# Centring retention's values in their weights, and four norms' column sums as split fp32r

## The chip, the cores and the metric

The kernel runs on one core of a Trainium2 chip. It uses the five engines of the core: TensorE (PE in the profile; its weight loads are PEld), VectorE (DVE), ScalarE (ACT), GpSimd (POOL), and SyncE (SP), which issues most of the DMAs. The metric is the device time of one execution in microseconds (us), as the median of several runs.

## The reference

Two blocks on one sequence of 1,024 positions and 1,024 channels, all in float32. The first block has two layers (a gated convolution, then dilated attention), each followed by a gated side branch; the second has one layer with neighbourhood attention (8 heads) and bidirectional retention (4 heads of 128 value channels) side by side, and an MLP. What the change touches is the mean square that each norm takes over the channels, and the norm behind retention, which takes a head's mean away:

```python
def rms_norm(x, g):
    y = x32 * lax.rsqrt(jnp.mean(x32 * x32, axis=-1, keepdims=True) + EPS)
    return y * g
...
def head_group_norm(y, gain):            # y: (batch, seq, heads, 128)
    mu = jnp.mean(y, axis=-1, keepdims=True)
    var = jnp.mean(jnp.square(y - mu), axis=-1, keepdims=True)
    y = (y - mu) * lax.rsqrt(var + EPS)
    return y.reshape(bsz, seq, heads * dv) * gain
...
    proj = h @ w_in[l]
    na_q, na_k, na_v, r_q, r_k, r_v, r_g = jnp.split(proj, splits, axis=-1)
    ret = bidirectional_retention(rq, rk, rv, ...)      # linear in rv
    ret = head_group_norm(ret, ret_norm_gain[l])
    ret_out = jax.nn.silu(r_g) * ret
```

## The kernel before

**Layout.** Activations stand transposed: 8 tiles of 128 channels by 1,024 positions, and X, the residual, stays in SBUF. A weight tile is 128 output channels for all 1,024 inputs, [128, 8, 128]. A product of full precision is made of three fp32r products: every operand is split in a rounded high part and the rest (HA, HB: high and low parts of the activations; w_hi, w_lo: of the weights), and hi by hi, lo by hi and hi by lo are added in PSUM. `linear(q, h)` (L878) makes one output tile from weight slot q (0 or 1) in 8 k-parts; each k-part is `products` (L866): 3 fp32r products times 2 halves of 512 positions. Products of plain fp32 operands need two passes where an fp32r product or a transpose needs one.

**Buffers.** PSUM has four tensors of 128x1024: AB (ps_A, ps_B), which `linear` takes in turn, and CD (ps_C, ps_D), taken in turn by everything else. A raw weight tile comes by DMA into w_raw[q]; POOL splits it (`split_weights`, L765: a cast to w_hi at L769, a subtraction to w_lo at L762) as soon as the product before it on that slot has ended; then SP loads the next.

**Order.** Each engine has its own program, and all order between them is by semaphores, written out by hand; the `Tally` class counts their values. An engine runs its list strictly in order, so a wait holds up all behind it.

**Norms.** The squares of the new X are added into ssum tile by tile by DVE (L2314), while the unscaled values times the gain already go into the products; the channels' sum comes from a product of ssum with a matrix of ones, in fp32 (`column_sums`, L889, called by `norm_stats`, L896). ScalarE makes rstd from it (L1490, L1492), and DVE multiplies by rstd when it evacuates a product (`evacuate`, L2354). `opening` (L900) is a stage's first `linear` with `norm_stats` behind it. It begins four stages: the side branches ple0 and ple1, the attention (norm1) and the second block's mixer (mix). In the attention, DVE goes on behind ssum with clearing qT and kT, the angles of the rotation, the evacuation of q and k and their squares' low parts (`square_lo`, L2557), which TensorE sums per head (`head_squares`) from k-part 4 of the third tile on.

**Neighbourhood attention.** Four times, a `linear` for the values, one for the keys, and `neighbourhood` (L1014): 8 units, and in each a k-part of the next tile, then the unit's scores into the other AB tensor. DVE takes the scores out into nsc with the bias and its largest value (`softmax_input`, L2808), ScalarE exponentiates, DVE normalises (L2816, L2819), TensorE turns and multiplies with the values, DVE stores (`take_out`, L2826). TensorE goes on to the tile behind the last unit when the last scores are out (`scores_out`), since it writes to the same PSUM tensor.

**Retention.** Two head pairs (i = 0, 1). Of each, six tiles: rq, rk, two values, two gates. rq of the first pair is the product carried by the last neighbourhood. DVE rotates rq and rk with operands that ScalarE swaps by DMA. The values of a head are turned to positions by channels: `centred_turn` (L1268) multiplies each 128x128 chunk by centre, the unit matrix less 1/128, in fp32, which turns it and takes away the mean over the head's channels at once. Since retention is linear in the values, the mean is then gone from its output. rkT is turned plainly (L1011, by a transpose). `decay_args` makes the table of decays, between ScalarE's exponentials.

## Time and profile before

| | us |
|---|---|
| median of 3 runs | 2422.59 |
| lowest, highest | 2422.40, 2423.52 |
| span of the profiled execution | 2422.7 |
| TensorE busy in it | 2373.7 (98%) |
| DVE, ScalarE, POOL busy | 1617.2 (67%), 1066.1 (44%), 942.1 (39%) |

The span is the time from the first to the last instruction of one execution under the profiler; it differs from the median by 0.1 us. Busy shares are a mean over stages. An engine's idle time costs something only where another waits for it; for TensorE, nearly always busy, every microsecond of waiting is listed with what ended it. Matmuls are pipelined, so a row's duration overlaps the next row's; the time of a product is the distance between starts.

### The profile page before, as it was taken

To read this page: it belongs to the slowest core of one execution; us is meant where nothing else is said; L and a number is where in the kernel's file an instruction comes from. 1 tells how busy PE (TensorE), PEld (TensorE's weight loads), DVE (VectorE), ACT (ScalarE), POOL (GpSimd) and SP (SyncE) were. 2 spreads that over 40 slices of the span, in tenths; PEclk is the share of its full clock that TensorE was granted. 3 is DMA by queue.
4 is the path that set the end of the run, shared out by engine and by line. 5 is a ranking of instruction groups with operands and counts; after the bars stand their busy time and mean duration, and the time that the engine had idled before them with its cause. 6 is when DMAs were issued, how large, how long until landed. Compare 5 with 4: busy or idle time off the path is not lost.

```text
span 2422.7 us, 31585 instructions
## 1 busy us (share of the span) xinstructions
PE 2373.7 (98%) x11548; PEld 1870.4 (77%) x11548; DVE 1617.2 (67%) x2013; ACT 1066.1 (44%) x1630; POOL 942.1 (39%) x528
## 2 busy tenths in 40 slices
PE   9999999999999999999999999999999999999997
PEld 6888648887777777777787777788877888788885
DVE  6999874467647466475856555455688777638985
ACT  5556572235545545456432333223353444444334
POOL 2899912332222222222233111212345455465553
PEclk9999999999999999999999999999999999999999
DMA  3111142221111111111132111221126666876773
GB/s 137 44 43 52 65 182 109 78 87 60 45 40 41 41 40 44 41 40 41 40 100 70 44 41 33 81 78 36 52 113 158 149 159 156 231 293 233 274 250 122
DMA packets 112228, 238.76 MB, mean 99 GB/s; under 512 B 42472, under 2 KB 45416, under 8 KB 112104
## 3 DMA queue, kind: packets, MB, share of 16 engines
q1 hardware_dynamic: 73152, 216.28, 27.8%
q10 hardware_dynamic: 38952, 20.76, 3.9%
q8 instruction: 86, 1.41, 0.2%
q14 instruction: 38, 0.31, 0.0%
HBM read 184.44 MB, written 46.27 MB: 95 GB/s over the span
## 4 chain that ended last, share of the span: by engine, by line
PE 82%; DVE 7%; POOL 3%; ACT 3%; issue 3%; DMA 1%; ACTq 0%; SPq 0%; DVEq 0%; POOLq 0%
PE ps_A L873 24%; PE ps_B L873 23%; PE ps_B L1373 8%; PE ps_A L1373 7%; PE ps_C L1373 4%; PE ps_D L1373 2%; POOL ta L795 1%; PE ps_C L893 1%; PE ps_B L966 1%; PE ps_B L1119 1%; PE ps_C L1011 1%; POOL accp L795 1%; PE ps_D L1011 1%; PE ps_D L1104 1%; PE ps_D L1092 1%
## 5 line engine op out<-in xcount | busy, mean ns | idle before, releaser
L769 POOL CAST w_hi<-w_raw 128x1024 fp32r<-128x1024 f32 x98 | 107.9, 1101 | 1090.4 <-issue 475.9
L762 POOL TENSOR_TENSOR w_lo<-w_raw,w_hi 128x1024 fp32r<-128x1024 f32 x124 | 304.4, 2456 | 50.1 <-ACT w_hi L1513 42.2
L838 POOL TENSOR_TENSOR down_w_lo<-d_raw,down_w_hi 128x512 fp32r<-128x512 f32 x112 | 178.2, 1612 | 141.8 <-ACT down_w_hi L2210 141.8
L873 PE MATMUL ps_A<-HA_hi,w_hi 128*128 128x512 f32 x640 | 201.6, 396 | 4.7 <-POOL w_lo L762 2.2
L873 PE MATMUL ps_B<-HA_hi,w_hi 128*128 128x512 f32 x640 | 202.4, 397 | 2.5 <-POOL w_lo L762 1.5
L873 PE MATMUL ps_A<-HA_lo,w_hi 128*128 128x512 f32 x640 | 197.6, 390 | 0.0
L873 PE MATMUL ps_B<-HA_lo,w_hi 128*128 128x512 f32 x640 | 197.4, 390 | 0.0
L873 PE MATMUL ps_A<-HA_hi,w_lo 128*128 128x512 f32 x640 | 197.3, 390 | 0.0
L873 PE MATMUL ps_B<-HA_hi,w_lo 128*128 128x512 f32 x640 | 197.3, 389 | 0.0
L873 PEld LDWEIGHTS ps_A<-HA_hi,w_hi 128*128 128x128 f32 x640 | 117.1, 188 | 30.8 <-issue 5.0
L873 PEld LDWEIGHTS ps_A<-HA_lo,w_hi 128*128 128x128 f32 x640 | 120.1, 188 | 25.6
L873 PEld LDWEIGHTS ps_B<-HA_lo,w_hi 128*128 128x128 f32 x640 | 120.1, 188 | 25.5
L873 PEld LDWEIGHTS ps_A<-HA_hi,w_lo 128*128 128x128 f32 x640 | 120.1, 188 | 25.5
L873 PEld LDWEIGHTS ps_B<-HA_hi,w_hi 128*128 128x128 f32 x640 | 116.8, 188 | 29.8 <-POOL w_lo L762 2.7
L873 PEld LDWEIGHTS ps_B<-HA_hi,w_lo 128*128 128x128 f32 x640 | 120.1, 188 | 25.4
L1550 ACT ACTIVATE tap_out<-ypad,act_dw 128x1024 f32<-128x1024 f32 x78 | 88.3, 1150 | 96.2 <-POOL accp L795 51.2
L832 POOL TENSOR_TENSOR up_w_lo<-a_raw,up_w_hi 128x512 fp32r<-128x512 f32 x64 | 90.9, 1421 | 77.6 <-ACT up_w_hi L2079 77.6
L3189 DVE TENSOR_TENSOR ht_lo<-t_raw,ht_hi 128x1024 fp32r<-128x1024 f32 x56 | 73.0, 1309 | 69.5 <-ACT ht_hi L2194 69.3
L2210 ACT CAST down_w_hi<-d_raw 128x512 fp32r<-128x512 f32 x112 | 64.5, 618 | 103.6 <-DVE d_raw L3208 39.7
L832 POOL TENSOR_TENSOR up_w_lo<-s,up_w_hi 128x512 fp32r<-128x512 f32 x48 | 72.9, 1520 | 84.3 <-ACT up_w_hi L2079 83.8
L873 PE MATMUL ps_A<-HB_hi,w_hi 128*128 128x512 f32 x320 | 101.8, 399 | 1.2 <-POOL w_lo L762 1.1
L873 PE MATMUL ps_B<-HB_hi,w_hi 128*128 128x512 f32 x320 | 101.7, 399 | 0.0
(489 smaller groups left out, 5926.6 us busy)
## 6 DMA issues: line engine op xcount, KB each, us to landing
w_raw<-w_dram SPq DMA_DIRECT2D x124, 512.0 KB, 3.3
d_raw<-w_dram SPq DMA_DIRECT2D x64, 512.0 KB, 4.5
t_raw<-u_dram SPq DMA_DIRECT2D x56, 512.0 KB, 5.7
a_raw<-w_dram SPq DMA_DIRECT2D x32, 512.0 KB, 7.7
u_dram<-b SPq DMA_DIRECT2D x56, 256.0 KB, 4.9
u_dram<-t SPq DMA_DIRECT2D x48, 256.0 KB, 7.0
X<-x_dram SPq DMA_DIRECT2D x16, 512.0 KB, 6.8
d_raw<-w_dram SPq DMA_DIRECT2D x32, 256.0 KB, 3.0
```

The source lines that it names most:

```text
L762: pool.tensor_tensor(w_lo[q][:, :, :], w_raw[q][:, :, :], w_hi[q][:, :, :].bitcast(F32), ALU.subtract).then_inc(S[f"w_ready{q}"], 1)
L769: pool.tensor_copy(w_hi[q][:, :, :], w_raw[q][:, :, :]).then_inc(S["w_rounded"], 1)
L795: pool.tensor_tensor(accp[u][:, :], (tap_out[0] if j == 0 else accp[u])[:, :], tap_out[(j + 1) % 2][:, :], ALU.add).then_inc(S["pool_tap"], 1)
L832: pool.tensor_tensor(lo[:, :, :], up_source(s), hi[:, :, :].bitcast(F32), ALU.subtract).then_inc(S["up_split"], 1)
L838: pool.tensor_tensor(lo[:, :, :], d_raw[i % 3][:, down_parts(x), :], hi[:, :, :].bitcast(F32), ALU.subtract).then_inc(S["down_split"], 1)
L873: op = pe.matmul(AB[b][:, cols], wt[:, w0 + k, :], act[:, k, cols], start=(first and k == ks[0] and step == 0), stop=(last and k == ks[-1] ...
L893: op = pe.matmul(ps[b][:, cols], m[:, :], src[:, cols], start=first, stop=last)
L1011: op = pe.transpose(CD[b][:, c * P:(c + 1) * P], src(c), ident[:, :])
L1373: op = pe.matmul(bank, a[:, k, :], b[:, k, :], start=(first and k == 0 and step == 0), stop=(k == KH - 1 and step == 2), skip_group_check= ...
L1550: act.activation(tap_out[j % 2][:, :], ypad[u][:, at:at + T], ACT.Identity, scale=act_dw[:, at:at + 1]).then_inc(S["tap_product"], 1)
L2210: act.copy(down_w[i % 3][j][0][:, :, :], d_raw[i % 3][:, down_parts(x), :]).then_inc(S["down_hi"], 1)
L3189: dve.tensor_tensor(dT[t % 4][1][:, ks, :], t_raw[k % 4][:, :, :], dT[t % 4][0][:, ks, :].bitcast(F32), ALU.subtract).then_inc(S["t_ready" ...
```

## The change

**Column sums.** For ple0, norm1, ple1 and mix, ScalarE casts ssum to fp32r (sum_hi), DVE subtracts it from ssum (sum_lo), and TensorE multiplies both with ones in fp32r (`split_stats`). The sum leaves `opening`; in ple0 and ple1 it stands at the head of the second tile, in norm1 and mix ahead of its third k-part.

**Values.** centre and `centred_turn` go; the values are turned by the plain `turn`. The mean over a head's 128 output channels is taken from the weights instead, in w_raw, before POOL splits them: `centre_weights` on DVE, two tiles each time, for the first pair behind unit 6 of the last neighbourhood, for the second behind the evacuation of rqT in the first pair. POOL's loop over these tiles is written out, with a wait for the centred tile in it.

**Semaphores.** Some are merged: the decay's load counts with the diffs, so that ScalarE's first exponential of the decays waits for all four loads; dw_loaded counts in vec_loaded. The renaming of rq_swapped and rk_swapped is left out below.

```diff
+        ones_r = rm.take("ones_r", [P, P], F32R)
+        w_mean = rm.take("w_mean", [P, 2, KT])
...
+        sum_lo, sum_hi = (Region(nc, (at, at + 4 * KB)).take(name, [P, T], F32R)
+                          for name, at in (("sum_lo", free0), ("sum_hi", free0 + 4 * KB)))
...
-            with n.loop(pool, (MLP_AT - W_TILES["conv_in"]) // 2 - 1, w_loaded0=16, w_loaded1=16, lin_done0=1,
+            with n.loop(pool, (RET_AT - W_TILES["conv_in"]) // 2 - 1, w_loaded0=16, w_loaded1=16, lin_done0=1,
                         lin_done1=1, w_rounded=2):
+                split_weights(0)
+                split_weights(1)
+            for pair in range(W_TILES["ret"] // 2):
+                for q in range(2):
+                    if pair % 3 == 1:
+                        pool.wait_ge(S["w_centred"], pair // 3 * 2 + q + 1)
+                    split_weights(q)
...
+            def split_stats():
+                n.next("ssum_added", KT)
+                pe.wait_ge(S["sum_split"], n.next("sum_split"))
+                b = take_cd()
+                for i, part in enumerate((sum_hi, sum_lo)):
+                    op = column_sums(part, ones_r, b, i == 0, i == 1)
+                op.then_inc(S["stats_done"], 1)
...
                 n.next("h_ready", KT)
-                norm_stats()
+
+            def stats_at(at):
+                return lambda k: split_stats() if k == at else None
...
                 opening(0, h)
-                linear(1, h)
+                linear(1, h, pre=stats_at(0))
...
             opening(0, HA)
-            linear(1, HA)
+            linear(1, HA, pre=stats_at(2))
...
-                linear(q ^ 1, HB, pre=rest)
+                linear(q ^ 1, HB, pre=rest or stats_at(2))
...
-                centred_turn(v_in[0])
+                value_turn(v_in[0])
...
+            def round_sum():
+                act.wait_ge(S["ssum_added"], n.now("ssum_added"))
+                act.copy(sum_hi[:, :], ssum[:, :]).then_inc(S["sum_hi"], 1)
...
-            act.wait_ge(S["decay_loaded"], 16)
+            act.wait_ge(S["diffs_loaded"], 4 * 16)
...
+            def split_sum():
+                after("sum_hi")
+                dve.tensor_tensor(sum_lo[:, :], ssum[:, :], sum_hi[:, :].bitcast(F32),
+                                  ALU.subtract).then_inc(S["sum_split"], 1)
...
+            def centre_weights(i):
+                for q in range(2):
+                    mean = w_mean[:, q, :]
+                    dve.wait_ge(S[f"w_loaded{q}"], 16 * ((RET_AT + 6 * i) // 2 + 2))
+                    step(dve.tensor_reduce(mean, w_raw[q][:, :, :], AX.X, ALU.add))
+                    dve.scalar_tensor_tensor(w_raw[q][:, :, :], mean.unsqueeze(2).to_broadcast([P, KT, P]), -1.0 / P,
+                                             w_raw[q][:, :, :], ALU.mult, ALU.add).then_inc(S["w_centred"], 1)
...
                     normalise(u)
+                    if j == PAIRS - 1 and u == 6:
+                        centre_weights(0)
...
                     evacuate(rqT[:, :], 0)
+                    centre_weights(i + 1)
```

On DVE, units 6 and 7 of the last neighbourhood before (nsc: scores, nst: a row's largest value and sum; ISA is the pass that takes scores out of ps_B):

```order
1046 L2819 TENSOR_SCALAR nsc_157<-nsc_157,nst 128x352 [waits dve_step]
1047 L2819 TENSOR_SCALAR nsc_157<-nsc_157,nst 128x352
1048 L2808 ISA nsc_158,nst<-ps_B,bias_154 128x384 [waits turned,scores_done]
1049 L2808 ISA nst 128x1
1050 L2808 ISA nsc_158,nst<-ps_B,bias_156 128x384
```

And the same place in the changed kernel:

```order
1050 L2867 TENSOR_SCALAR nsc_161<-nsc_161,nst 128x352 [waits dve_step]
1051 L2867 TENSOR_SCALAR nsc_161<-nsc_161,nst 128x352
1052 L2815 TENSOR_REDUCE w_mean<-w_raw_54 128x8 [waits w_loaded0]
1053 L2816 SCALAR_TENSOR_TENSOR w_raw_54<-w_mean,w_raw_54 128x1024 [waits dve_step]
1054 L2815 TENSOR_REDUCE w_mean<-w_raw_55 128x8 [waits w_loaded1]
1055 L2816 SCALAR_TENSOR_TENSOR w_raw_55<-w_mean,w_raw_55 128x1024 [waits dve_step]
1056 L2856 ISA nsc_162,nst<-ps_B,bias_158 128x384 [waits turned,scores_done]
```

Four passes over the two value tiles now stand between unit 6's probabilities and unit 7's scores.

On DVE, the end of the sum and the beginning of the attention (norm1) before:

```order
303 L2314 TENSOR_TENSOR ssum<-ssum,sq 128x1024 [waits ssum_added]
304 L182 REGISTER_ALU
305 L182 COMPARE_AND_BRANCH
306 L2705 MEMSET qT 128x1024
307 L2705 MEMSET kT 128x1024 [waits dve_step]
```

And in the changed kernel:

```order
304 L2344 TENSOR_TENSOR ssum<-ssum,sq 128x1024 [waits ssum_added]
305 L182 REGISTER_ALU
306 L182 COMPARE_AND_BRANCH
307 L2355 TENSOR_TENSOR sum_lo<-ssum,sum_hi 128x1024 [waits sum_hi]
308 L2743 MEMSET qT 128x1024
```

The subtraction, with its wait for ScalarE's cast, stands ahead of everything that DVE does for the attention.

## Rows read from the trace of the kernel before

**Rows 1.** The page, part 4: the chain that ended last, by engine.
```profile
PE 82%; DVE 7%; POOL 3%; ACT 3%; issue 3%; DMA 1%; ACTq 0%; SPq 0%; DVEq 0%; POOLq 0%
```

**Rows 2.** Timeline, mix: start, duration, engine, line, operation, count [idle before <- releaser].
```profile
1303.23 1.88 PE L893 MATMUL ps_C<-ssum,ones 128*128 128x512 f32 x4
1305.41 0.62 PE L873 MATMUL ps_B<-HB_lo,w_hi 128*128 128x512 f32 x2
```

**Rows 3.** Timeline, beginning of the attention (norm1), four engines.
```profile
549.30 1.22 DVE L2314 TENSOR_TENSOR ssum<-ssum,sq 128x1024 f32<-128x1024 f32 x1
...
552.82 2.91 DVE L2581 CAST turns<-pos_i 128x1024 f32<-128x1024 int32 x1
...
569.99 1.23 DVE L2557 TENSOR_TENSOR k_lo<-k_sq,k_hi 128x1024 fp32r<-128x1024 f32 x1
...
561.63 1.05 ACT L1705 CAST q_hi<-q_sq 128x1024 fp32r<-128x1024 f32 x1
...
564.29 1.36 POOL L769 CAST w_hi<-w_raw 128x1024 fp32r<-128x1024 f32 x1 [9.11 <-issue]
...
571.27 0.73 PE L893 MATMUL ps_C<-k_hi,head_r 128*128 128x512 f32 x2 [0.78 <-DVE k_lo L2557]
```

**Rows 4.** Timeline, TensorE, retention: turns of the values and of rkT.
```profile
1559.88 1.10 PE L1011 MATMUL ps_C<-ident,rkT 128*128 128x128 f32 x8 [1.35 <-DVE rkT L2912]
...
1645.30 1.95 PE L1273 MATMUL ps_D<-centre,mix 128*128 128x128 f32 x16
1647.08 1.04 PE L1011 MATMUL ps_C<-ident,rkT 128*128 128x128 f32 x8
1647.87 0.71 PE L873 MATMUL ps_B<-HB_hi,w_hi 128*128 128x512 f32 x2
```

**Rows 5.** Timeline, beginning of ple1: the last add and the sum.
```profile
1209.69 1.23 DVE L2314 TENSOR_TENSOR ssum<-ssum,sq 128x1024 f32<-128x1024 f32 x1
...
1214.43 1.88 PE L893 MATMUL ps_D<-ssum,ones 128*128 128x512 f32 x4
```

**Rows 6.** Timeline, retention: DVE and POOL at the same time.
```profile
1636.89 3.41 DVE L2911 TENSOR_TENSOR r_m<-r_m,rsin 128x1024 f32<-128x1024 f32 x1
...
1635.88 3.34 POOL L762 TENSOR_TENSOR w_lo<-w_raw,w_hi 128x1024 fp32r<-128x1024 f32 x1
```

**Rows 7.** Timeline, last neighbourhood, units 6 and 7: DVE, TensorE, POOL.
```profile
1518.52 0.72 DVE L2819 TENSOR_SCALAR nsc<-nsc,nst 128x352 f32<-128x352 f32 x2
1519.85 0.56 DVE L2808 CUSTOM_DVE_ANT_0 nsc<-ps_B,bias 128x384 f32<-128x384 f32 x1 [0.62 <-PE ps_B L1058]
...
1520.34 0.55 DVE L2808 CUSTOM_DVE_ANT_0 nsc<-ps_B,bias 128x384 f32<-128x384 f32 x1
...
1521.17 0.71 PE L873 MATMUL ps_B<-HB_hi,w_hi 128*128 128x512 f32 x2
...
1519.13 1.04 POOL L769 CAST w_hi<-w_raw 128x1024 fp32r<-128x1024 f32 x1 [24.35 <-PE ps_A L873]
```

**Rows 8.** Timeline, one row; and groups by line: busy us, mean ns | idle before.
```profile
1201.31 1.28 DVE L2307 SCALAR_TENSOR_TENSOR HA_lo<-X,vec,HA_hi 128x1024 fp32r<-128x1024 f32 x1 [0.23 <-ACT HA_hi L1502]
...
L2611 DVE TENSOR_REDUCE least<-st_x 128x16 f32<-128x48 f32 x4 | 0.9, 214 | 0.0
```

**Rows 9.** Timeline, DVE, retention, behind the evacuation of rqT.
```profile
1618.70 1.23 DVE L2942 TENSOR_TENSOR r_m<-r_m,sd_sq 128x1024 f32<-128x1024 f32 x1 [8.01 <-ACT sd_sq L2053]
```

**Rows 10.** Timeline, TensorE, MLP; and a stretch: length, busy by engine, PEclk, DMA, GB/s.
```profile
1824.73 0.51 PE L1373 MATMUL ps_B<-ht_hi,up_w_hi 128*128 128x512 f32 x1 [1.90 <-DVE b L3072]
...
1826.00:1829.40 3.40, 3.40 (x10) 2.64 (x9) 1.99 (x4) 2.72 (x6) 3.40 (x3) 0.52 1.03 186
```

**Rows 11.** Timeline, retention's first pair: DVE and POOL.
```profile
1537.86 1.03 DVE L2874 COPY lg<-lg 64x4 f32<-64x4 f32 x2 [1.32 <-ACT lg L1973]
...
1556.64 1.22 DVE L2911 TENSOR_TENSOR r_m<-r_m,rsin 128x1024 f32<-128x1024 f32 x1
...
1556.91 1.84 POOL L769 CAST w_hi<-w_raw 128x1024 fp32r<-128x1024 f32 x1 [7.35 <-issue]
```

More of the change, by code:

```diff
@@ L389, in build @@
         TAB_X, TAB_Z = RET_HEADS * P, 2 * RET_HEADS * P
-        centre = rr.take("centre", [P, P])
         lg = rr.take("lg", [P, 4, RET_HEADS])
@@ L1266, in chunk, with value_turn @@
                 return t[rows, c * P:(c + 1) * P]
-            def centred_turn(v):
-                b = take_cd()
-                pe.wait_ge(S["centre_ready"], 1)
-                for c in range(BLOCKS):
-                    op = pe.matmul(chunk(CD[b], c), chunk(v, c), centre[:, :], start=True, stop=True)
-                op.then_inc(S["v_turned"], 1)
+            def value_turn(v):
+                turn(lambda c: chunk(v, c), BLOCKS)[1].then_inc(S["v_turned"], 1)
             def chunk_states(h):
@@ L1530, in _ @@
             act.wait_ge(S["ssum_added"], DVE_SQUARES - 1)
-            act.dma_start(dw_sb[:, :, :], dw).then_inc(S["dw_loaded"], 16)
+            act.wait_ge(S["ones_loaded"], 16)
+            act.copy(ones_r[:, :], ones[:, :])
+            act.dma_start(dw_sb[:, :, :], dw).then_inc(S["vec_loaded"], 16)
             norm_stats()
@@ L1686, in _ @@
                 .then_inc(S["pos_loaded"], 16)
+            round_sum()
             norm_stats()
@@ L1908, in _ @@
             load_rows(1)
+            round_sum()
             norm_stats()
@@ L1957, in _ @@
                 act.wait_ge(S[f"cd_free{b}"], n.now(f"cd_free{b}"))
-            act.dma_start(lg[:, 0:2, :], decay).then_inc(S["decay_loaded"], 16)
+            act.dma_start(lg[:, 0:2, :], decay).then_inc(S["diffs_loaded"], 16)
             at = (BLOCKS - 1) * P
@@ L2014, in _ @@
                 act.wait_ge(S[f"ab_free{b}"], n.now(f"ab_free{b}"))
-                swap_halves("rq_swapped", qs, rqT)
+                swap_halves("q_swapped", qs, rqT)
                 after_ab()
-                swap_halves("rk_swapped", r_m1[0], rkT)
+                swap_halves("k_swapped", r_m1[0], rkT)
                 pass_ab(2)
@@ L2702, in pair @@
                 gated(j)
+            split_sum()
             for dst in (qT, kT):
@@ L2867, in decay_args @@
             def decay_args():
-                dve.scalar_tensor_tensor(centre[:, :], ones[:, :], -1.0 / P, ident[:, :], ALU.mult,
-                                         ALU.add).then_inc(S["centre_ready"], 1)
                 after("gamma_ready", 2)
@@ L2877, in decay_args @@
                     dve.tensor_copy(lg[high, 3, e::2], lg[high, 1, 1 - e::2])
-                after("diffs_loaded", 3 * 16)
+                after("diffs_loaded", 4 * 16)
                 apart, toward = steps[:, 0:P], steps[:, P:2 * P]
@@ L2951, in _ @@
                     decay_args()
-                turned_pair("rq_swapped", rqT, qs, "rq_ready")
+                turned_pair("q_swapped", rqT, qs, "rq_ready")
                 evacuate(mix[:, i * 2 + PAIRS, :], 0)
-                turned_pair("rk_swapped", rkT, r_m1[0], "rk_ready")
+                turned_pair("k_swapped", rkT, r_m1[0], "rk_ready")
                 evacuate(mix[:, i * 2 + 1 + PAIRS, :], 1)
```

13 lines of the change are left out of this document (9 added, 4 removed).

## The prediction

> **What bounds the kernel now.** I read the page's chain of waits first: 82% of the span runs through TensorE [rows 1], so TensorE time saved counts in full and a TensorE wait added counts in full, unless a wait that is already there takes it up. Then the list of TensorE's own waits: there are few, and the change stands beside two of them, one of 0.78 us at the first attention tiles, before 571.27 [rows 3], and one of 1.35 us in the retention stage [rows 4]. So the question is what the change takes off TensorE, and where the added VectorE (DVE) work makes TensorE wait. The profiled execution's span is 2422.7 us and the median of the runs 2422.6, so the two can be taken as one; I sum against 2422.6.
>
> **Column sums of four norms (ple0, norm1, ple1, mix).** From the sum's first pass at 1303.23 to the products' second pair at 1305.41 are 2.18 us; one pair of products in it takes 0.455 us, so the four fp32 passes of the sum take 1.73 us [rows 2]. In fp32r the sum is four passes as well (high and low part, two halves each), at the 0.227 us of a product, 0.91 us together: 0.82 us less for each norm.
>
> The new chain is: last add into ssum, ScalarE's cast to sum_hi (1.05 us, as the cast of the same shape [rows 3]), DVE's subtraction (1.22 us), TensorE. For ple1 the last add ends at 1210.92, so the low part is there at about 1213.3, and TensorE asks at 1214.43 [rows 5]: hidden with 1.1 us to spare; uncovered it would cost those 2.3 us. ple0 has more room. For mix the sum is asked for two k-parts (2.7 us) after 1303.23 [rows 2], and the masks and biases that DVE does behind the subtraction have idle time after them. Three norms: -2.5 us.
>
> **norm1 is different**, because DVE has a full list behind the sum. Its last add ends at 550.52 [rows 3]. DVE waits for the cast until 551.6 and subtracts until 552.9; the low part is ready 2.4 us after the last add and the sum's new place is two k-parts (2.7 us) behind the old one, so TensorE doesn't wait there. But the whole list behind it (clearing qT and kT, the angles, the evacuations, the low parts q_lo and k_lo) is 2.3 us late. The conversion of the positions took 2.91 us at 552.82 [rows 3], of which I put over 2 us down to standing still beside a subtraction of GpSimd (POOL); so about 1.0 of the 2.3 us vanishes there and 1.35 us stay. Then POOL's next split, 564.29 before [rows 3], comes 0.8 us earlier, because TensorE does, and DVE's list is later: its cast and subtraction (some 1.0 and 2.4 us) now fall ahead of q_lo instead of beside the evacuation of k_in. Laid out operation by operation, k_lo ends at about 574.1 where it ended at 571.22, and TensorE goes on at 574.2 instead of 571.27 [rows 3]. So here the 0.82 us are lost and 2.9 us come on top. Bounds: +1.4 (only the first shift) and +3.3 (nothing vanishes at the conversion). I take +2.9, since the two-SBUF operations in this trace do stand still beside POOL [rows 6].
>
> **Turns of the values.** The product with centre takes 16 passes and 1.78 us (1645.30 to 1647.08), a plain turn 8 passes and 0.79 us (1647.08 to 1647.87) [rows 4]: 0.99 us less, four times. The first of the four is followed by the 1.35 us wait for rkT [rows 4], whose chain (ScalarE's loads, decay arguments, swaps) doesn't get shorter; that wait grows by 0.99 us and nothing is won. Three count: -3.0 us. Nothing else that I find waits in their place: the second turn is followed by score products whose operands have been there for microseconds.
>
> **Centring in the last neighbourhood unit.** This is the term that decides. After the probabilities of unit 6 (1518.52 + 0.72 = 1519.24) DVE goes to the scores of unit 7 at 1519.85 and gives them free at 1520.9; TensorE starts the rk tile at 1521.17, in the very bank that those scores stood in [rows 7]. Only 0.6 us of idle time is there. Now two reductions and two products over 128x1024 stand between. A product of this kind (scalar_tensor_tensor) is 1.28 us, a reduction of 48 elements a partition 214 ns [rows 8]; no row shows one of 1,024. I bound it by 0.9 us (the 1.28 us less a third) and 1.3 us, and take 1.2: 0.16 us fixed, worked out from the short one, and 1.06 us for the elements, as in the 1.22 us passes (such as [rows 9]). Two tiles: about 4.85 us, from 1519.15 to 1524.0. Scores free at 1525.0, TensorE at 1525.1 instead of 1521.17: +3.95 us (bounds 3.3 and 4.3). What is queued behind on DVE: unit 7's scores and probabilities, the evacuation of rqT, both needed microseconds later. ScalarE's loads for the retention stage wait for unit 7's output, which comes from TensorE, so the rkT chain shifts along and its wait doesn't take the stall up. POOL's split of the first value tile, 1519.13 before [rows 7], waits for the centred tile until 1521.7; TensorE needs it at about 1539: hidden, at 13 us.
>
> The second centring stands in an idle stretch of DVE of 8.01 us before 1618.70 [rows 9]; 4.85 us fit: nothing. POOL's split there is late by 4 us against 14: nothing. ScalarE now waits for all four loads instead of the decay's before its first exponential, about 0.75 us later; but the first copies of lg behind it took 1.03 us for four columns each, from 1537.86 [rows 11], standing beside POOL's subtraction, so I take 0, bounds 0 and 0.7. Dropping the centre matrix (0.28 us) is ahead of the same stand: 0. The rounded ones and the unrolled POOL loop lie in idle time: 0.
>
> **TensorE's clock.** In the products of the MLP TensorE stood still 1.90 us before 1824.73, and from 1826.0 to 1829.4 the granted clock was 0.52, its 1.2 GHz level, with 10 products in 3.40 us [rows 10]: (1 - 0.52) x 3.40 = 1.6 us lost. After the 1.35 us wait [rows 4] it stayed at 2.4 GHz. The change makes two waits much longer than 1.90: 3.95 us at 1521, and some 4.6 us in two pieces at 569 to 574. TensorE is the bound behind both, so I count 1.6 us for each, 3.3 together (bounds 0 and 4.8). The wait for rkT becomes 1.35 + 0.99 = 2.3 us, a little over the one that was followed by the low level; with one case to go by I take half of it, 0.8.
>
> **Sum.** -2.5 + 2.9 - 3.0 + 3.95 + 3.3 + 0.8 = +5.5 us: 2428.1 us. What a measurement of this kernel can tell from no change is about 0.2%, 4.8 us.
>
> **Rivals.**
>
> *POOL gets ahead of DVE (slower still).* DVE operations with two SBUF inputs and POOL's passes take turns in this trace: rkT's product with the sines lasted 3.41 us at 1636.89, until POOL's w_lo (1635.88, 3.34) had ended [rows 6]. In the centring, POOL starts its cast when the first tile is centred, and DVE asks for its second product some 1.15 us later, just as that cast ends. By my durations DVE is ahead of POOL's w_lo by 0.1 us; if the reduction takes over 1.3 us it is behind, and waits 2.4 us more: 2430.5. The same can happen at rkT, where DVE (1556.64) is ahead of POOL's cast (1556.91) by 0.27 us [rows 11]: 2.7 us more, 2430.8, or 2433.2 with both. Chance 0.2.
> The Trainium skill, "SBUF — State Buffer", section "Who interferes with whom", says that whichever of the two issues first holds the shared ports for the whole instruction, that a tensor_reduce never takes them on trn2, and that an operation with two SBUF inputs does. By that rule, the trace agrees at 1636.89, the reductions are safe and the second product alone is at stake, which is this rival.
>
> *The centring and the splits are covered (faster).* If TensorE didn't need the scores' bank before DVE is back, and norm1's list had slack, all that is left is 3.3 us from the sums and 3.0 us from the turns: 2416.3. It decides at one point, whether DVE's detour at 1519 ends within about 0.9 us of its old time. For it speaks only that DVE is idle 1 to 2 us in each unit; against it that the idle time lies ahead of unit 7 only with 0.6 us. Chance 0.1.
>
> *The clock stays at 2.4 GHz.* The stalls come as worked out, and no low stretch follows: 2422.6 + 1.4 = 2424.0. For it: only one low stretch in the trace; against it: the waits are twice as long as the one before it. Chance 0.15.
>
> **How the numbers follow.** My forecast has 0.55, its own range 2425.5 to 2429.8 (norm1 by its bounds, none to two and a half low stretches). The range over all: 2421.5 to 2432.5; it leaves out the covered case and the case of both collisions with POOL. Slower by over 0.2% means above 2427.4: all of the POOL rival and about 0.6 of the forecast, 0.53. Faster: 0.10. Within: 0.37.
>
> **What would show it.** Right: a TensorE wait of about 4 us for DVE's nst (L2856 after) just ahead of the rk tile; two low-clock stretches of 3.4 us; the k sum of the first head_squares some 3 us later against the tile before it; column sums of 0.9 us; turns of 0.8 us; DVE idle before L2990 shrunk from 8.0 to about 3. Wrong: TensorE going on at once after unit 7, which would leave only gains; or reductions far from 1.2 us, which move the stall by twice the difference.

## The result and the profile after

| | before | after |
|---|---|---|
| median, us | 2423.28 | 2428.05 |
| lowest, highest, us | 2422.40, 2425.45 | 2425.90, 2434.80 |
| span of the profiled execution, us | 2422.7 | 2426.7 |

The ratio is 1.0019, 95% interval [1.001, 1.0028]: 4.8 us slower, just about the smallest difference that can be told from none. Both kernels ran eight times in this comparison. One slow execution of after, 7354.05 us, whose cause is not known, is left out of the ratio and of the highest value and counts in the median alone, which is 2427.95 without it. The other seven runs of after spread three times as wide as those of before, and that turns out to be part of the answer.

The page after, parts 1 and 4. TensorE is still 98% busy and the chain's shares are those of [rows 1], so every row below is about where TensorE stands still or runs slowly.

```profile
PE 2368.9 (98%) x11516; PEld 1868.4 (77%) x11516; DVE 1631.2 (67%) x2024; ACT 1071.1 (44%) x1635; POOL 951.9 (39%) x528
...
PE 82%; DVE 7%; POOL 3%; ACT 3%; issue 3%; DMA 1%; ACTq 0%; SPq 0%; DVEq 0%; POOLq 0%
```

TensorE's waits after (line, what it waited for: us in total, times, longest). The first is new. The second was 0.78 us [rows 3], the third 1.35 us [rows 4].

```profile
PE ps_B L885 <- DVE nst L2856: 3.6, 1, 3.6
PE ps_C L905 <- DVE k_lo L2594: 3.5, 1, 3.5
...
PE ps_C L1035 <- DVE rkT L2960: 2.5, 1, 2.5
```

**The stall at the last neighbourhood unit.** Timeline after, DVE, POOL and TensorE; it answers to [rows 7]. Between the probabilities of unit 6 (L2867) and the scores of unit 7 (L2856) stand two reductions of 1.21 us and two products of 1.22 us, 4.78 us from 1522.24 to 1527.02. POOL's cast starts behind the first centred tile, and its subtraction (1526.02) behind DVE's second product (1525.87), 0.15 us apart: DVE stayed ahead.

```profile
1521.61 0.72 DVE L2867 TENSOR_SCALAR nsc<-nsc,nst 128x352 f32<-128x352 f32 x2
1522.24 1.21 DVE L2815 TENSOR_REDUCE w_mean<-w_raw 128x8 f32<-128x1024 f32 x1
1523.48 1.22 DVE L2816 SCALAR_TENSOR_TENSOR w_raw<-w_mean,w_raw 128x1024 f32<-128x1024 f32 x1
1524.63 1.21 DVE L2815 TENSOR_REDUCE w_mean<-w_raw 128x8 f32<-128x1024 f32 x1
1525.87 1.22 DVE L2816 SCALAR_TENSOR_TENSOR w_raw<-w_mean,w_raw 128x1024 f32<-128x1024 f32 x1
1527.02 0.55 DVE L2856 CUSTOM_DVE_ANT_0 nsc<-ps_B,bias 128x384 f32<-128x384 f32 x1
...
1526.02 3.30 POOL L765 TENSOR_TENSOR w_lo<-w_raw,w_hi 128x1024 fp32r<-128x1024 f32 x1
...
1528.11 1.22 PE L885 MATMUL ps_B<-HB_hi,w_hi 128*128 128x512 f32 x2 [3.60 <-DVE nst L2856]
```

**norm1.** Timeline after, beginning of the attention; it answers to [rows 3]. DVE waits for ScalarE's cast and subtracts (550.92). The conversion of the positions took 1.64 us where it had taken 2.91, but q_lo took 3.42 us, because POOL's subtraction had begun 0.39 us before it. k_lo ended at 572.69, and TensorE, which asked at 569.28, stood still for 3.46 us.

```profile
550.92 1.22 DVE L2355 TENSOR_TENSOR sum_lo<-ssum,sum_hi 128x1024 fp32r<-128x1024 f32 x1 [1.12 <-ACT sum_hi L1522]
...
554.45 1.64 DVE L2618 CAST turns<-pos_i 128x1024 f32<-128x1024 int32 x1
...
564.61 3.42 DVE L2594 TENSOR_TENSOR q_lo<-q_sq,q_hi 128x1024 fp32r<-128x1024 f32 x1
...
571.46 1.23 DVE L2594 TENSOR_TENSOR k_lo<-k_sq,k_hi 128x1024 fp32r<-128x1024 f32 x1 [0.44 <-ACT k_hi L1734]
...
564.22 2.72 POOL L765 TENSOR_TENSOR w_lo<-w_raw,w_hi 128x1024 fp32r<-128x1024 f32 x1
...
572.74 1.22 PE L905 MATMUL ps_C<-k_hi,head_r 128*128 128x512 f32 x2 [3.46 <-DVE k_lo L2594]
```

**The clock.** Stretches of after: length, TensorE busy (count), granted clock, DMA share, GB/s. At both waits the clock fell to 0.50, the 1.2 GHz level, for 6.8 us each time: from 571.3 to 578.1 and from 1527.1 to 1533.9, so that it was already low for the last 1.4 and 1.1 us of the waits. The 0.60 and 0.57 below are means over stretches that are a little longer. Behind the MLP's wait of 1.9 us, where the kernel before had its only low stretch [rows 10], it did not. The last row is for later: 1,005 products in 228 us of the MLP.

```profile
569.30:571.30 2.00, 0.00 (x0) 1.00 0.21 84
571.40:578.10 6.70, 5.36 (x13) 0.50 0.28 40
...
572.50:579.50 7.00, 6.76 (x19) 0.60 0.24 34
1526.50:1534.50 8.00, 6.39 (x16) 0.57 0.19 66
1824.00:1840.00 16.00, 14.09 (x62) 1.00 0.73 179
1850.00:2078.00 228.00, 228.00 (x1005) 1.00 0.61 151
```

**The retention stage.** Timeline after. A turn of values takes 0.87 us to the next, where the product with centre took 1.78 us [rows 4]. DVE's idle time ahead of L2990, with the second centring in it, has shrunk from 8.01 us [rows 9] to 3.23.

```profile
1569.76 1.09 PE L1035 MATMUL ps_C<-ident,rkT 128*128 128x128 f32 x8 [2.46 <-DVE rkT L2960]
...
1654.27 1.03 PE L1035 MATMUL ps_D<-ident,mix 128*128 128x128 f32 x8
1655.14 1.04 PE L1035 MATMUL ps_C<-ident,rkT 128*128 128x128 f32 x8
...
1627.67 1.23 DVE L2990 TENSOR_TENSOR r_m<-r_m,sd_sq 128x1024 f32<-128x1024 f32 x1 [3.23 <-ACT sd_sq L2083]
```

**The account.** The table gives, for the same TensorE instruction in each profiled execution, its start less its start in the first trace of the kernel before. A change from row to row is what that stretch cost or gave. "Late", "fp32" and "both" are kernels of the next section.

| instruction (start before) | before, 2nd | after | after, 2nd | late | fp32 | both |
|---|---|---|---|---|---|---|
| second tile behind ple0's sum, 464.71 | -0.40 | -0.71 | -0.89 | -0.99 | -0.76 | -0.92 |
| norm1, k sum, 571.27 | -0.40 | 1.47 | 1.28 | 1.18 | -0.78 | -0.95 |
| attention, 620.39 | -0.39 | 4.32 | 3.09 | 3.06 | -0.78 | -0.96 |
| attention, 899.75 | -0.18 | 4.62 | 3.34 | 3.29 | -0.73 | -1.01 |
| behind ple1's sum, 1216.61 | -0.20 | 3.91 | 2.71 | 2.60 | -1.53 | -1.79 |
| behind mix's sum, 1307.70 | -0.19 | 3.08 | 1.89 | 1.77 | -2.36 | -2.62 |
| rk tile, 1521.17 | -0.30 | 6.94 | 5.80 | 1.71 | 1.43 | -2.62 |
| turn of rkT, 1559.88 | -0.29 | 9.88 | 7.43 | 4.40 | 6.12 | -2.54 |
| second pair's scores, 1660.73 | -0.32 | 7.15 | 4.66 | 4.18 | 5.92 | -5.28 |
| MLP, 1825.31 | -0.28 | 7.21 | 4.69 | 4.57 | 6.22 | -5.23 |
| MLP, 1853.80 | -0.26 | 5.53 | 3.00 | 4.14 | 5.81 | -6.90 |
| MLP, 2058.36 | -0.26 | 4.24 | 1.71 | 2.85 | 4.51 | -8.20 |
| last norm's sum, 2405.46 | -0.97 | 3.96 | 0.60 | 1.83 | 4.10 | -8.23 |

### The profile page after: what moved, and what is told of

The parts are those of the page before. It is cut to its first block, busy times and chain, and to the rows that moved or that the text cites. A ratio compares the mean times of both kernels' runs of the same rounds, so it can differ in the third digit from the quotient of the medians.

```text
span 2426.7 us, 31507 instructions
## 1 busy us (share of the span) xinstructions
PE 2368.9 (98%) x11516; PEld 1868.4 (77%) x11516; DVE 1631.2 (67%) x2024; ACT 1071.1 (44%) x1635; POOL 951.9 (39%) x528
## 4 chain that ended last, share of the span: by engine, by line
PE 82%; DVE 7%; POOL 3%; ACT 3%; issue 3%; DMA 1%; ACTq 0%; SPq 0%; DVEq 0%; POOLq 0%
PE ps_A L885 24%; PE ps_B L885 24%; PE ps_B L1393 8%; PE ps_A L1393 7%; PE ps_C L1393 4%; PE ps_D L1393 2%; POOL ta L798 1%; PE ps_C L905 1%; PE ps_B L990 1%; PE ps_B L1143 1%; PE ps_C L1035 1%; PE ps_D L1035 1%; POOL accp L798 1%; PE ps_D L1128 1%; PE ps_D L1116 1%
## 5 line engine op out<-in xcount | busy, mean ns | idle before, releaser
L844 POOL TENSOR_TENSOR up_w_lo<-s,up_w_hi 128x512 fp32r<-128x512 f32 x48 | 79.5, 1659 | 71.1 <-ACT up_w_hi L2109 70.0
```

Of the source, the lines that this page charges most:

```text
L844: pool.tensor_tensor(lo[:, :, :], up_source(s), hi[:, :, :].bitcast(F32), ALU.subtract).then_inc(S["up_split"], 1)
```

## The experiments

My theory: the stall at unit 7 and the one for k_lo make up the loss, each with a low clock behind it, over gains of 5 to 6 us. Rivals: the low clock isn't the waits'; the cost lies elsewhere in the retention stage.

Ratios below are against the kernel before, run beside each kernel; differences from after are between medians of different comparisons. After's interval was [1.001, 1.0028]. Those of the kernels with one edit overlap or touch it, so their medians alone prove little and the readings rest on their traces; the kernels with both edits are clear of it.

### Centring the first pair late

```diff
-                    if j == PAIRS - 1 and u == 6:
-                        centre_weights(0)
...
                     evacuate(rqT[:, :], q)
+                    centre_weights(0)
                 take_out(6)
```

> The changed kernel with one move: the first pair of value tiles is centred behind the evacuation of rqT, where VectorE stands idle, instead of between the probabilities of unit 6 and the scores of unit 7. Everything is still computed. Theory (the detour of VectorE makes the stall at 1521 to 1528 us, and the stall brings the low clock behind it): TensorE's wait of 3.6 us for nst ahead of the rk tile goes, and the 6.8 us at the low clock behind it with it, 3.9 + 2.8 = 6.7 us less than the changed kernel, about 2421.3 us. Rival (the low clock there is not the stall's): only 3.9 us less, 2424.1. Second rival (with this low stretch gone, the one in the MLP that the kernel before had at 1826 comes back, with 1.6 us, and what the changed kernel was faster by in the MLP's products, 1.5 to 2 us, goes): 2424.4 to 2425.

Measured: 2425.17 us (2419.56 to 2431.93), ratio 1.0007 [0.9997, 1.0017]. The stall is gone: from mix's sum to the rk tile the shift goes from 1.77 to 1.71 us, where after went from 3.08 to 6.94. But the time fell by 2.9 us, not 6.7, and the executions spread by 12 us. The trace shows what took the gain. Timeline of this kernel, DVE, POOL and TensorE:

```profile
1558.89 2.06 DVE L2958 TENSOR_TENSOR r_m<-r_m,rsin 128x1024 f32<-128x1024 f32 x1
1560.98 3.25 DVE L2959 TENSOR_TENSOR rkT<-rkT,r_m 128x1024 f32<-128x1024 f32 x1
...
1558.62 1.24 POOL L772 CAST w_hi<-w_raw 128x1024 fp32r<-128x1024 f32 x1 [7.37 <-issue]
...
1564.28 1.97 PE L1035 MATMUL ps_C<-ident,rkT 128*128 128x128 f32 x8 [4.94 <-DVE rkT L2959]
```

And the same place in the changed kernel:

```profile
1566.52 1.22 DVE L2959 TENSOR_TENSOR r_m<-r_m,rsin 128x1024 f32<-128x1024 f32 x1
1567.77 1.94 DVE L2960 TENSOR_TENSOR rkT<-rkT,r_m 128x1024 f32<-128x1024 f32 x1
...
1566.59 2.04 POOL L772 CAST w_hi<-w_raw 128x1024 fp32r<-128x1024 f32 x1 [7.36 <-issue]
```

Where DVE starts its product with the sines first, it takes 1.22 us and the addition 1.94; where POOL's cast starts first, they take 2.06 and 3.25, and TensorE waits 4.94 us for rkT, not 2.46. The shift from the rk tile to rkT is +2.69 us here and +0.08 with both edits, where DVE was first by 0.19 us. This is my first rival, at the second of its two places, with the price that I had given it (2.7 us), but in another kernel: in the changed one DVE was first by 0.07 us. A low stretch followed the long wait (4.40 to 6.00 at the scores behind it, although a turn's 0.9 us was gained between), and the MLP's was back, as the second rival had it (4.57 to 4.14, where after went from 7.21 to 5.53); the MLP's pace, which that rival gave up too, stayed. The 3.9 us of the stall were won and mostly lost again at a place that none of this run's theories had named.

### norm1's sum in plain fp32

```diff
-            opening(0, HA)
-            linear(1, HA, pre=stats_at(2))
+            opening(0, HA)
+            norm_stats()
+            linear(1, HA)
...
-            round_sum()
             norm_stats()
...
-            split_sum()
             for dst in (qT, kT):
```

> The changed kernel, but norm1's column sums in plain fp32 as before the change: no cast, no subtraction, no low part. Everything is still computed. Theory (VectorE's list behind norm1's sum was late, k_lo came late, and the wait of 3.46 us for it brought a low clock): the shift over norm1 of 1.47 + 0.82 = 2.3 us and the 3.1 us of the low clock go, the 0.82 us of the sum come back: 2428.05 - 1.5 - 3.1 = 2423.5 us; the wait ahead of the k sum is 0.8 us again. Rival (the low clock is not the wait's): 2426.6 us with the low clock still near 573 us.

Measured: 2423.72 us (2421.30 to 2429.10), ratio 1.0001 [0.9992, 1.001]; expected was 2423.5. Timeline, TensorE: the wait for k_lo is the old one again, and the "fp32" column stays at -0.78 through the attention, where after went from -0.71 to 4.32. The low clock at 573 us is gone with the wait, so it was the wait's.

```profile
570.49 0.73 PE L905 MATMUL ps_C<-k_hi,head_r 128*128 128x512 f32 x2 [0.79 <-DVE k_lo L2594]
```

The profiled execution, at 2428.6 us, is among the slowest of this kernel: POOL's cast was first by 0.62 us at rkT (wait 5.3 us, as in the kernel above), and of 11 executions three lie at 2428.6 to 2429.1 and eight at or below 2424.7. The trace supports no more than that this kernel meets both cases.

### Both edits

> Both edits together: first centring behind rqT, norm1's sums in plain fp32. Everything is still computed. Theory (the two costs are apart and add up): 2428.05 - 6.7 - 4.6 = 2416.8 us, faster than the kernel before by 6 us or more; that is the three sums (2.5) and three to four turns (3.0 to 4) without their costs. Rival (low stretches come back elsewhere, 1.6 us each, and the MLP's pace falls back): 2418.5 to 2420.5 us.

Measured: 2418.48 us (2415.47 to 2423.28), ratio 0.998 [0.9971, 0.9989]; theory 2416.8, rival 2418.5 to 2420.5. The two costs are apart and each has its own cure: the kernel is 5.5 us faster than before and, between two comparisons, 9.6 us faster than after. The trace of the profiled execution (2416.29) shows no low stretch until the last 9 us of the span, where every trace has one. Its column gives the change's own gains apart from its costs: three sums -0.8 each and three turns -0.9 each, 5.3 us together, with the first turn's gain lost in the wait for rkT. The rest of its -8.2 is not the sums' or the turns': 1.7 us is the MLP's low stretch, not met here, and 1.3 us the MLP's pace, treated below. The theory's 2416.8 fits this execution; the median stands at the lower edge of the rival, and no slower execution of this kernel was traced.

```profile
1557.34 1.09 PE L1035 MATMUL ps_C<-ident,rkT 128*128 128x128 f32 x8 [2.35 <-DVE rkT L2958]
```

### One of the two first tiles centred late

```diff
-            def centre_weights(i):
+            def centre_weights(i, tiles=range(2)):
...
-                for q in range(2):
+                for q in tiles:
...
-                        centre_weights(0)
+                        centre_weights(0, [0])
...
                     evacuate(rqT[:, :], q)
+                    centre_weights(0, [1])
```

> The changed kernel with only one of the two first value tiles centred ahead of unit 7's scores, the other behind the evacuation of rqT. Everything is still computed. Theory (the stall is VectorE's added time less the 0.6 to 1 us that it had to spare): 2.43 us of detour instead of 4.86, a stall of about 1.2 to 1.5 us, 2.4 us less; after a wait as short as the one of 1.35 us for rkT in the kernel before the clock stays at 2.4 GHz, another 2.8 us less: about 2422.8 us. Rival (any wait here brings the low clock): 2425.6 us. Second rival (POOL's cast gets ahead of VectorE in the shorter list): up to 1 us more.

Measured: 2424.47 us (2423.05 to 2427.68), ratio 1.0005 [0.9996, 1.0014]. The stall scales with DVE's detour: 2.4 us less of it, 2.38 us less wait. No low clock followed this wait of 1.22 us; one of 3.4 us did follow the wait for k_lo, still 3.46 us here. The median is 3.6 us below after where the theory had 5.2; why the rest is missing stays open.

```profile
1524.76 0.73 PE L885 MATMUL ps_B<-HB_hi,w_hi 128*128 128x512 f32 x2 [1.22 <-DVE nst L2856]
```

### The decays' load with its own semaphore

The change also made ScalarE wait for four loads instead of one ahead of the exponential that starts the decay tables. From the issue of the first load to that exponential it is 3.57 us in the kernel before, 4.62 in the changed one, 4.94 with late centring and 5.30 with norm1 in fp32; the last two are those in which POOL was first. So I undid it, once over both edits and once in the changed kernel alone.

```diff
-            act.dma_start(lg[:, 0:2, :], decay).then_inc(S["diffs_loaded"], 16)
+            act.dma_start(lg[:, 0:2, :], decay).then_inc(S["decay_loaded"], 16)
...
-            act.wait_ge(S["diffs_loaded"], 4 * 16)
+            act.wait_ge(S["decay_loaded"], 16)
...
-                after("diffs_loaded", 4 * 16)
+                after("diffs_loaded", 3 * 16)
```

> The kernel of both edits, with one part of the change undone besides: ScalarE's first exponential of the retention stage waits for the load of the decays alone again, not for all four loads. Everything is still computed. Theory (the shared semaphore makes ScalarE, and VectorE's decay arguments behind it, late by 0.7 to 1.7 us, and whoever starts first of VectorE's product with the sines and GpSimd's cast of the next weights keeps the other waiting): from the start of the first load to the exponential 3.6 us as in the kernel before, not 4.3 to 5.3; VectorE ahead of the cast in the profiled run; the wait for rkT 1.4 to 2.3 us and never 5; the median 0 to 2 us below that of both edits (2418.5), and no execution above 2421. Rival (VectorE's list, not ScalarE, sets the time, and the spread is the clock's alone): the same median and the same spread, 2415.5 to 2423.3 us.

> The changed kernel with one part undone: ScalarE's first exponential of the retention stage waits for the load of the decays alone, as before the change. Everything is still computed. Theory (in the profiled execution of the changed kernel VectorE was ahead of GpSimd's cast by 0.07 us only; with the exponential 0.7 to 1.7 us earlier it is always ahead): from the start of the first load to the exponential about 3.7 us; wait for rkT 2.3 to 2.5 us; both low stretches (near 573 and 1528 us) stay; median 0 to 2 us below the changed kernel's 2428.05, so 2426 to 2428, and none of the executions above 2430. Rival (this wait has nothing to do with the spread): the same median, single executions up to 2434.8.

Measured over both edits: 2415.53 us (2414.92 to 2419.26), ratio 0.9971 [0.996, 0.9981], the fastest kernel of this study, 8 us below the kernel before. In the changed kernel: 2426.94 us (2425.25 to 2428.26), ratio 1.0015 [1.0006, 1.0024]. The exponential is early again (3.72 and 3.88 us), DVE is first by 0.27 and 0.29 us where it had been by 0.19 and 0.07, and no execution is above the bound that the theories gave, 2421 and 2430. The first kernel still has two groups, five executions at 2414.9 to 2415.7 and three at 2418.7 to 2419.3, so not all of the spread is gone. The medians fall by 3.0 and 1.1 us with intervals that overlap those of the kernels without the edit.

The traces together say more than each pair. In the 12 in which DVE's list ahead of rkT isn't reordered, the time from the load to the exponential is 3.5 to 3.9 us where it waits for one load, and 4.25 to 5.3 us where it waits for four. Up to 4.4 us DVE is first by 0.27 to 0.30 us, the second trace of the changed kernel among them (4.41 us, 0.27). Beyond that the lead falls one for one: 0.19 at 4.49, 0.07 at 4.62, and POOL is first by 0.27 at 4.94 and by 0.62 at 5.30. So the shared semaphore can lose the race for DVE, but does so only in executions in which the loads take long. How much of the medians it is stays unsettled. ScalarE and TensorE over both edits, timeline:

```profile
1529.93 0.36 ACTq L1988 DMA_DIRECT2D lg<-decay_dram  x1
...
1533.65 0.21 ACT L2001 ACTIVATE lg<-lg 128x8 f32<-128x8 f32 x1 [8.29 <-DMA lg<-decay_dram]
...
1557.28 1.09 PE L1035 MATMUL ps_C<-ident,rkT 128*128 128x128 f32 x8 [2.26 <-DVE rkT L2958]
```

### rkT ahead of the mix tile

Over both edits, in the first pair of heads:

```diff
-                evacuate(mix[:, i * 2 + PAIRS, :], 0)
+                if i:
+                    evacuate(mix[:, i * 2 + PAIRS, :], 0)
                 turned_pair("k_swapped", rkT, r_m1[0], "rk_ready")
+                if i == 0:
+                    evacuate(mix[:, i * 2 + PAIRS, :], 0)
```

> The kernel of both edits, with VectorE doing the three passes that turn rkT ahead of the evacuation of the first tile for mix, in the first of the two pairs of heads. Everything is still computed. Theory: rkT is ready one evacuation (1.13 us) earlier, TensorE's wait for it falls from 2.35 to about 1.2 us; the product with the sines starts 1.1 us earlier, so that GpSimd's cast never gets ahead; median 1.1 to 2.5 us below that of both edits (2418.5): 2416 to 2417.4 us, with a smaller spread. Rival (the bank of the mix tile, freed 3.4 us later, is what TensorE asks for next): the wait moves to the next tile, no gain or up to 2 us more.

Measured: 2417.98 us (2415.46 to 2421.66), ratio 0.9978 [0.9969, 0.9988]: no gain, as the rival had it, but for a simpler reason. The tile evacuated is the value tile whose turn stands ahead of rkT's on TensorE. The wait moved there and grew by 1.1 us. A low stretch of 3.4 us followed it (0.50 from 1558.7 to 1562.1), which the profiled execution with both edits didn't have; its 1.7 us are about the 1.6 us between the two spans. Timeline of TensorE:

```profile
1557.44 1.10 PE L1035 MATMUL ps_D<-ident,mix 128*128 128x128 f32 x8 [3.46 <-DVE mix L2390]
1558.37 1.61 PE L1035 MATMUL ps_C<-ident,rkT 128*128 128x128 f32 x8
```

### fp32r kept in norm1, head sums later

As the last kernel, with norm1's sum as in the change, and

```diff
-            linear(0, HA, pre=lambda k: head_squares() if k == 4 else None)
+            linear(0, HA, pre=lambda k: head_squares() if k == 6 else None)
```

> As the kernel with rkT first, but norm1's sums stay in fp32r as in the changed kernel, and the head sums of norm1's third tile stand behind six k-parts instead of four (2.7 us later). Everything is still computed. Theory (what fp32r cost in norm1 is only VectorE's lateness with k_lo, which TensorE waited 3.46 us for): TensorE asks 2.7 us later, waits 0.5 to 1 us, and no low clock follows; the 0.82 us of the shorter sum are won: 0.8 us below the kernel with rkT first, 2415.2 to 2416.6 us. Rival (the norms of q and k, later by 2 to 2.7 us themselves, are asked for without slack behind): the wait comes back some microseconds on, 1 to 2.7 us, and the median is 0 to 2 us above that kernel's.

Measured: 2425.71 us (2424.54 to 2427.45), ratio 1.0008 [0.9999, 1.0017], 7.7 us above the kernel with rkT first; the theory wanted 0.8 below. The wait for k_lo shrank to 1.06 us as expected. It came back some 20 us on, for q_in, timeline of the kernel and its waits:

```profile
572.76 0.73 PE L905 MATMUL ps_C<-k_hi,head_r 128*128 128x512 f32 x2 [1.06 <-DVE k_lo L2594]
...
579.71 3.31 DVE L2600 TENSOR_TENSOR k_in<-k_in,cosT 128x1024 f32<-128x1024 f32 x1
...
589.34 2.70 DVE L2611 TENSOR_TENSOR kT<-k_in,k_root 128x1024 f32<-128x1024 f32 x1
```

```profile
PE ps_B L1143 <- DVE q_in L2390: 4.8, 2, 4.3
```

DVE's late list meets POOL's next passes one operation further on, k_in's product stands still beside POOL's subtraction (3.31 us), and the first scores of the attention wait for all of it. Behind this wait of 4.26 us the clock was low from 593.4 to 596.8, and stretches of the same length came in the retention stage, behind a wait of 2.5 us for the first tile of mix, and in the MLP; the trace of the kernel with rkT first has only the one in the retention stage. The wait and the two further stretches are 4.3 + 2 x 1.7 = 7.7 us and so most of the 8.3 us between the two spans. So DVE's lateness, not the place of the head sums, is what has to go.

### Second traces

> The changed kernel once more, for a second trace. Everything is computed. Theory A (how long the clock stays low behind a wait depends on the wait alone): 6.8 us twice again, behind the waits of 3.46 and 3.60 us. Theory B (it varies from one execution to the next, as 6.8 us in the changed kernel and 3.4 us in the kernel with late centring behind the same wait of 3.46 us have it): 3.4 or 6.8 us at each. The wait for rkT is 2.5 us if VectorE is ahead of GpSimd's cast, 4.9 to 5.3 us if it is behind.

> The kernel before, once more, for a second trace. Everything is computed. Theory A (the slower pace of the MLP's products from 1850 to 2078 us, 1.3 us over the five kernels with the change, belongs to the kernel): the same 1.3 us show again against every kernel with the change. Theory B (it belongs to that one execution): the pace is that of the changed kernels. For the low clock behind the MLP's wait of 1.91 us: seen again if the wait alone brings it, absent if it is met in some executions only.

The changed kernel's second execution took 2425.15 us, with the same three waits (3.5, 3.6, 2.3 us). Its stretches, same columns as above:

```profile
569.10:572.40 3.30, 0.00 (x0) 1.00 0.20 62
572.50:575.80 3.30, 3.25 (x8) 0.50 0.34 50
...
572.50:579.50 7.00, 6.95 (x24) 0.76 0.23 34
1526.50:1534.50 8.00, 7.53 (x37) 0.79 0.20 66
```

Theory B holds. The same wait of 3.46 us was followed by a loss of 2.85 us in one execution (1.47 to 4.32) and of 1.8 us in the other (1.28 to 3.09); behind unit 7 it is 2.9 us and 1.6 us (from 6.94 to 9.88 and 5.80 to 7.43, with 0.1 to 0.2 for rkT in both). That is 2.3 of the 3.3 us between the two executions; 0.8 of the rest comes behind 2058.36 (last two rows of the table) and isn't explained. The kernel before met its one low stretch in the MLP again, at the same place.

The length goes with the moment at which the clock fell. Ahead of the last 12 us of the span the 14 traces have 19 low stretches, 6 of 6.8 us and 13 of 3.4 us. In the six the clock fell while TensorE still stood, 1.05 to 1.8 us before it went on; in the thirteen it fell at most 0.4 us before that or up to 1.4 us behind it. Above it is 571.3 against TensorE's start at 572.74 (6.8 us), and 572.5 against 572.55 (3.4 us). That moment shifts between executions of one kernel, as these two show for the same wait.

### GpSimd's loop taken apart, and plain turns alone

In all kernels with the change the MLP's products are 1.3 us faster over 1850 to 2078 than in both traces of before (rows 1853.80 and 2058.36 of the table). I tried two parts of the change on the kernel before. The second of the two kernels leaves the centring out, so the values keep their mean.

```diff
-            with n.loop(pool, (MLP_AT - W_TILES["conv_in"]) // 2 - 1, w_loaded0=16, w_loaded1=16, lin_done0=1,
+            with n.loop(pool, (RET_AT - W_TILES["conv_in"]) // 2 - 1, w_loaded0=16, w_loaded1=16, lin_done0=1,
...
+            for pair in range(W_TILES["ret"] // 2):
+                for q in range(2):
+                    split_weights(q)
+            with n.loop(pool, (MLP_AT - RET_END) // 2, w_loaded0=16, w_loaded1=16, lin_done0=1, lin_done1=1,
+                        w_rounded=2):
+                split_weights(0)
+                split_weights(1)
```

> The kernel before, with only GpSimd's loop of weight splits taken apart as the change does it (a loop up to the retention stage, its 12 pairs written out, a loop for the rest), without any centring. Everything is still computed. Theory (the 1.3 us that the MLP's products from 1850 to 2078 us took more in both traces of the kernel before come from where GpSimd's code lies): those 1.3 us go, every other marker stays within 0.3 us. Rival: nothing changes, the 1.3 us have another cause.

```diff
...
-                    op = pe.matmul(chunk(CD[b], c), chunk(v, c), centre[:, :], start=True, stop=True)
-                op.then_inc(S["v_turned"], 1)
+                turn(lambda c: chunk(v, c), BLOCKS)[1].then_inc(S["v_turned"], 1)
...
```

> The kernel before, with the four turns of the values done as plain turns (8 passes each, not 16) and the centre matrix left out. The centring of the values is left out altogether, so their mean isn't taken off. Theory: the first turn's gain is lost in the wait for rkT, which grows from 1.35 to 2.3 us; the other three give 0.9 us each: 2.7 us less than the kernel before (2423.3), 2420.6. Second question, the pace of the MLP's products from 1850 to 2078 us (1.3 us slower in all traces of the kernel before than in those with the change): if TensorE's shorter program is its cause, those 1.3 us go as well, 2419.3; if it is not, only the 2.7 us. The low clock of 1.6 us behind the MLP's wait of 1.91 us may be met or not, as the kernel before met it twice and the kernel with GpSimd's loop taken apart didn't: 2419 to 2420.6 for that.

The loop taken apart: 2422.21 us in its one execution; the pace is unchanged (-1.53 at 1853.80 and at 2058.36), but the MLP's low stretch, 1.4 us, is not there, although the wait of 1.9 us is. The plain turns: 2421.47 us against 2424.15 of before beside them, ratio 0.999 [0.9981, 0.9999]. rkT's turn is not earlier, the scores behind are by 0.92 us, the second pair's by 2.73 us: 0 + 3 x 0.91, as the theory had it. The pace again stays. Counts of products in one stretch, the kernel before and then both edits with the decays' semaphore:

```profile
1850.00:2078.00 228.00, 228.00 (x999) 1.00 0.62 153
```

```profile
1850.00:2078.00 228.00, 228.00 (x1006) 1.00 0.62 156
```

What in the change gives the MLP these 7 products more in 228 us is open; it is neither of these two parts.

## Why the prediction came out right

The forecast was 2428.1 us, measured were 2428.05, and the mechanism was the one forecast: a stall at unit 7, a stall for k_lo, a low clock at each. But the agreement to 0.1 us is luck. The forecast was +5.5 us on 2422.6; the kernel before came out at 2423.28 in the comparison, so that the measured change is +4.8. And the clock's term was too small, while 3.0 us of gain in the MLP were not in the sum at all. The forecast's own range didn't follow from its terms either: with norm1 at its lower bound and no low stretch they give about 2422.5, not 2425.5.

**Three norms, -2.5.** Measured in after -0.71 (with the start of the kernel, which varies by some tenths), -0.71 and -0.83. Right.

**norm1, +2.9.** Measured +2.2 (from -0.71 to 1.47). Which operation would collide with POOL (q_lo, not the conversion) was right; k_lo ended 0.7 us earlier than laid out, counted from the start of the stage. The bounds, 1.4 and 3.3, held it.

**Turns, -3.0.** Measured -2.7, in after and with the turns alone: a plain turn takes 0.87 us where the next turn follows it (1654.27 to 1655.14); the 0.79 us of [rows 4] were from a turn to a weight product. That the first of the four is lost in the wait for rkT was right.

**Centring, +3.95.** Measured +3.86 (3.08 to 6.94). The reduction, which I had to bound by 0.9 and 1.3 us, takes 1.21. That the second centring and POOL's later splits cost nothing was right.

**Clock, +3.3 and +0.8.** The term that was mis-sized. I took the 1.6 us of the one low stretch in the trace for each. The profiled execution lost 2.85 and some 2.75 us, 5.6 together; the second one 1.8 and 1.5, 3.3 together. Behind the 2.46 us for rkT nothing followed in either, where I had put half a stretch. In the profiled execution the clock cost 5.6 us against my 4.1. What I lacked was that a low stretch can last 6.8 us as well as 3.4, by when the clock falls within the wait.

**What the sum didn't have.** The MLP's low stretch of before was not met in the changed kernel (7.21 to 5.53, -1.7), and the products' pace gave 1.3 us (5.53 to 4.24). I had taken everything behind the retention stage as unchanged. These 3.0 us and norm1's 0.7, against 1.5 more for the clock and 0.3 to 0.5 each for turns, sums and small shifts, bring +5.5 down to the +4.0 of the profiled spans.

**ScalarE's wait for four loads, 0 with bounds 0 and 0.7.** The exponential came 1.05 us later, and little of it reached TensorE (+0.2 from the stall to rkT). But in this execution it ate most of the 0.27 us by which DVE was ahead of POOL's cast [rows 11], down to 0.07. I had named this race as a rival at 0.2 without seeing that this very edit feeds it. It wasn't lost in either trace of the changed kernel; in two other kernels with the same shared wait it was, at the price named. The Trainium skill, "SBUF — State Buffer", section "Who interferes with whom", says that of DVE and POOL the one that issues first holds the shared ports for the whole instruction; the traces agree, 1.22 us against 2.06 for the same product by who was first. They agree too with what the prediction quotes of tensor_reduce: DVE's reduction took its 1.21 us and POOL's cast beside it its usual 1.04.

**Covered after all, clock stays.** The first fell with the trace: TensorE asks for the scores' bank at once. The second fell as well, in both traces.

## What to carry to other kernels

A few microseconds of work moved onto a partly idle engine cost what they overrun at the one point where the bound engine waits for what is queued behind; look for the place with a long idle stretch, here some 5 us later in the same list, before choosing by the stage's mean load. Where two engines hold each other up, as DVE and POOL do here, and arrive within 0.3 us of each other, price both outcomes, and ask of every other edit, a merged semaphore too, whether it moves either of them. A wait of 3.5 us with the low clock behind it cost 5 to 6.5 us here, and a single trace shows only one of the sizes that this can take.

## What the runs showed of the hardware

- The same wait in the same kernel came with a low clock of two lengths, 0.50 for 6.8 us in one execution and for 3.4 us in another. It was the longer one in all six stretches in which the clock fell over 1 us before TensorE went on, the shorter one in the 13 others. Over the 14 traces a low stretch came with all 13 waits of 3.5 us and more, with one of the eight of 2.2 to 2.5 us in the retention stage, and with the MLP's wait of 1.9 us in five; none came with a shorter wait, such as the 1.70 us ahead of 1152.38, which all 14 traces have.
- The executions of one kernel spread by 3 us (the kernel before, in the first comparison), 12 us (late centring) and 4.3 us (the fastest). The mean granted clock falls as the time grows: 0.999 at 2419.56 us and 0.993 at 2431.93 with late centring, 0.997 at 2425.90 and 0.993 at 2434.80 in after. So low clock is a large part of the spread; a lost race at rkT adds its wait and, in both traces that have it, a low stretch of 6.8 us.
- A reduction of 128x1024 in fp32 takes DVE 1.21 us, about as long as its product over the same tile (1.22 us); POOL's cast beside it takes its usual 1.04 us.
